# Half-width last tiles and first tiles around three stage borders, in a float32 hybrid layer: the order of matmuls, weight splits, statistics and gate rows is changed

## The reference

```
h = rms_norm(x) * (1 + sc0) + sh0
x = x + 0.5 * g0 * rms_norm(swiglu(h, f_in[0], f_out[0]))      # d_ff 2816
h = rms_norm(x) * (1 + sc1) + sh1
y = token_mixer(h)     # h @ w_in, then mLSTM (8 heads) and attention (16/4 heads), gates, @ w_out
x = x + g1 * rms_norm(y)
h = rms_norm(x) * (1 + sc2) + sh2
x = x + 0.5 * g2 * rms_norm(swiglu(h, f_in[1], f_out[1]))
```

## Time and profile before

| | |
|---|---|
| median of 3 executions | 1885.39 us (1884.95 to 1885.58) |
| the profiled execution | 1890.55 us, span in the trace 1888.7 us |
| busy share of the span | PE 96%, DVE 51%, ACT 35% |
| mean granted TensorE clock | 0.984 of full speed |
| chain that ended last | PE 88%, DVE 5%, ACT 4% |

### The profile page before, as it was taken

The page is one execution under the profiler, slowest core; times in us unless marked ns, Lnnn a source line. Parts: engine busy times, 40 slices in busy tenths (PEclk is TensorE's granted clock), DMA queues, the critical chain, the costliest instruction groups (busy, mean ns, idle before and its releaser), DMA issues.

```text
span 1888.7 us, 31491 instructions
## 1 busy us (share of the span) xinstructions
PE 1808.8 (96%) x12852; PEld 1750.3 (93%) x12852; DVE 967.3 (51%) x1636; ACT 655.9 (35%) x1145; POOL 0.2 (0%) x4
## 2 busy tenths in 40 slices
PE   7899999999988999899999999979999999999997
PEld 6899999999977999899999888879989999999996
DVE  4665555656365334455537888865463212222235
ACT  3422222212364222443435555443652222221233
POOL 0000000000000000000000000000000000000000
PEclk9999999999999999999999999999999999999998
DMA  7444444443213123232243211102312222222221
GB/s 300 154 153 126 156 132 146 131 136 120 70 34 134 57 68 92 87 92 74 91 134 111 66 40 53 38 19 79 134 45 68 77 78 70 75 78 78 66 58 56
DMA packets 52285, 178.35 MB, mean 94 GB/s; under 512 B 8513, under 2 KB 11091, under 8 KB 51411
## 3 DMA queue, kind: packets, MB, share of 16 engines
q1 hardware_dynamic: 52179, 176.86, 29.3%
HBM read 162.28 MB, written 13.90 MB: 93 GB/s over the span
## 4 chain that ended last, share of the span: by engine, by line
PE 88%; DVE 5%; ACT 4%; issue 2%; DMA 0%; SPq 0%; DVEq 0%; ACTq 0%
PE psum L525 21%; PE psum L526 21%; PE psum L527 21%; PE psum L938 2%; PE psum L948 2%; PE psum L913 2%; PE psum L563 1%; PE psum L565 1%; PE psum L564 1%; PE psum L620 1%; PE psum L609 1%; PE psum L653 1%; PE psum L830 1%; PE psum L654 1%; PE psum L655 1%
## 5 line engine op out<-in xcount | busy, mean ns | idle before, releaser
L525 PE MATMUL psum<-h_hi,whi 128*128 128x320 f32 x2096 | 659.6, 315 | 7.9 <-ACT mq L1249 4.5
L527 PE MATMUL psum<-h_hi,wlo 128*128 128x320 f32 x2096 | 650.7, 310 | 0.0
L526 PE MATMUL psum<-h_lo,whi 128*128 128x320 f32 x2096 | 650.7, 310 | 0.0
L1460 DVE TENSOR_TENSOR wlo<-raw,whi 128x1024 fp32r<-128x1024 f32 x191 | 233.2, 1222 | 650.6 <-ACT whi L1042 650.5
L525 PEld LDWEIGHTS psum<-h_hi,whi 128*128 128x128 f32 x2096 | 396.7, 189 | 13.6 <-issue 10.7
L526 PEld LDWEIGHTS psum<-h_lo,whi 128*128 128x128 f32 x2096 | 396.6, 189 | 0.6
L527 PEld LDWEIGHTS psum<-h_hi,wlo 128*128 128x128 f32 x2096 | 396.2, 189 | 0.0
L1042 ACT CAST whi<-raw 128x1024 fp32r<-128x1024 f32 x191 | 199.3, 1044 | 357.9 <-PE psum L527 343.7
L525 PE MATMUL psum<-g_hi,whi 128*128 128x320 f32 x512 | 158.5, 310 | 0.0
L526 PE MATMUL psum<-g_lo,whi 128*128 128x320 f32 x512 | 158.2, 309 | 0.0
L527 PE MATMUL psum<-g_hi,wlo 128*128 128x320 f32 x512 | 158.2, 309 | 0.0
(11 more groups left out here) (329 smaller groups left out, 2619.3 us busy)
## 6 DMA issues: line engine op xcount, KB each, us to landing
raw<-in_w_ffn_in SPq DMA_DIRECT2D x88, 512.0 KB, 3.5
raw<-in_w_mix SPq DMA_DIRECT2D x77, 512.0 KB, 3.9
mw<-in_w_mod SPq DMA_DIRECT2D x28, 768.0 KB, 4.5
raw<-in_w_ffn_out SPq DMA_DIRECT2D x32, 512.0 KB, 3.5
mw<-in_w_mod SPq DMA_DIRECT2D x4, 2048.0 KB, 19.4
gate<-gate_keep SPq DMA_DIRECT2D x24, 320.0 KB, 4.6
mw<-in_w_mod SPq DMA_DIRECT2D x14, 512.0 KB, 3.6
gate_keep<-gate SPq DMA_DIRECT2D x20, 320.0 KB, 4.5
```

Of the source, the lines that this page charges most:

```text
L525: mm(out, whi[t.slot][:, k, :], hi[:, k, cols], start=(k == 0), stop=False)
L526: mm(out, whi[t.slot][:, k, :], lo[:, k, cols], start=False, stop=False)
L527: last = mm(out, wlo[t.slot][:, k, :], hi[:, k, cols], start=False, stop=(k == nk - 1))
L1460: tt(lo[:, 0:nk, :], raw[t.raw][:, 0:nk, :], hi[:, 0:nk, :].bitcast(F32), ALU.subtract).then_inc(raw_free, 1)
```

## The change

Four edits. (a) In `last_tiles` on PE, tiles 0 and 1 are interleaved in their first half: k = 0 to nk - 2 of tile 0, the same of tile 1, then the last k of tile 0, the last k of tile 1. (b) ACT and DVE split the weights one tile further ahead: tile 2 before the loop, then tile i + 3 ahead of the eviction of tile i; the order of the second halves becomes 4, 5, 6, 7, 0, 1, 2, 3, and the kept weights change places (tiles 2 and 3 now in `xhi`/`xlo`). (c) For l < 2, `half_stats_y(l, 1)` is issued inside `first_four`, behind k = 3 of the two interleaved tiles, and all eight calls of `half_stats(l, 1)` behind u = 2. (d) Gate rows: ACT does the Exp behind the eviction of tile 2 and the Ln behind that of tile 3; DVE does `forget()` ahead of the split of tile 5.

```
-SECOND = (2, 3, 4, 5, 0, 1, 6, 7)
+SECOND = (4, 5, 6, 7, 0, 1, 2, 3)
+Y_STATS = 3
...
-            if u >= 6:
-                return xhi[u - 6], xlo[u - 6]
-            return held_r3[u - 4] if l == 1 and u >= 4 else held[u - 2]
+            if u < 4:
+                return xhi[u - 2], xlo[u - 2]
+            return held_r3[u - 6] if l == 1 and u >= 6 else held[u - 4]
...
             def last_tiles(l, base, nk, hi, lo, ready, first):
-                for u in range(KC):
-                    half_tile(l, u, u, base, 0, nk, hi, lo, ready if u == 0 else None, first)
+                for ks in (range(nk - 1), range(nk - 1, nk)):
+                    for u in range(2):
+                        if ks.start == 0:
+                            half_wait(l, u, u, base, 0)
+                        half_passes(l, u, u, base, 0, ks, nk, hi, lo, ready if u == 0 else None, first)
+                for u in range(2, KC):
+                    half_tile(l, u, u, base, 0, nk, hi, lo)
...
-                half_stats_y(l, 1)
+                if l == 2:
+                    half_stats_y(l, 1)
...
                             last = first_half(l, base, u, h, range(k, k + 1), u == 0)
                             if h == 1 and k == KC - 1:
                                 last.then_inc(tile_done, 1)
+                        if h == 0 and k == Y_STATS:
+                            half_stats_y(l, 1)
...
                         if h == 0:
-                            half_stats(l, 1, range(4 * u - 8, 4 * u - 4))
+                            if u == 2:
+                                half_stats(l, 1, range(KC))
...
+                split(w[2], weights(l, 2, base)[0], w[0].n + 2, nk)
                 for i in range(KC):
-                    u = i + 2
...
+                    u = i + 3
                     if u < KC:
                         split(w[u], weights(l, u, base)[0], w[0].n + 2, nk)
                     square_y(l, i, 0, base)
...
-                if l == L_GATE + 1:
+                if l == L_GATE + 2:
                     act.wait_ge(row_d, 1)
                     fn(t1[:, :, :], t1[:, :, :], ACT.Exp, scale=-1.0).then_inc(row_a, 1)
+                if l == L_GATE + 3:
                     act.wait_ge(row_a, 1)
                     fn(t1[:, :, :], t1[:, :, :], ACT.Ln, bias=epsc[0:H, 1:2]).then_inc(row_a, 1)
...
+                split(w[2], weights(l, 2, base), nk)
                 for i in range(KC):
-                    if i + 2 < KC:
-                        split(w[i + 2], weights(l, i + 2, base), nk)
+                    if i + 3 < KC:
+                        split(w[i + 3], weights(l, i + 3, base), nk)
                     take(i, 0)
...
+                if l == 1:
+                    forget()
                 if l < 2:
                     split(Tile(T_MIX + l + 4))
```

More of the change, by code:

```diff
@@ L174, in build @@
         whole = KC * P * 4
-        held = [[at(f"held{u}_{n}", [P, KC, P], F32R, h_at + (u - 2) // 2 * KC * row + (u % 2 * 2 + n) * whole)
-                 for n in range(2)] for u in range(2, 6)]
+        held = [[at(f"held{u}_{n}", [P, KC, P], F32R, h_at + (u - 4) // 2 * KC * row + (u % 2 * 2 + n) * whole)
+                 for n in range(2)] for u in range(4, KC)]
         held_r3 = [[at(f"held_r3_{u}_{n}", [P, KC, P], F32R, r3 + (u % 2 * 2 + n) * whole)
-                    for n in range(2)] for u in range(4, 6)]
+                    for n in range(2)] for u in range(6, KC)]
         xtok = at("xtok", [P, NT, D], F32, h_at)
@@ L548, in project_two, with half_wait @@
                             last.then_inc(tile_done, 1)
-            def half_tile(l, i, u, base, h, nk, hi, lo, ready=None, first=0):
+            def half_wait(l, i, u, base, h):
                 t, w = Tile(base + i), Tile(base + u)
-                wh, wl = weights(l, u, base)
                 if h == 0:
@@ L558, in half_tile, with half_passes @@
                     pe.wait_ge(ev[t.slot], t.pair)
-                out = half_out(t.slot, h)
-                for k in range(nk):
+            def half_passes(l, i, u, base, h, ks, nk, hi, lo, ready=None, first=0):
+                wh, wl = weights(l, u, base)
+                out = half_out(Tile(base + i).slot, h)
+                for k in ks:
                     if ready is not None:
@@ L565, in half_tile @@
                     last = mm(out, wl[:, k, :], hi[:, k, HCOLS[h]], start=False, stop=(k == nk - 1))
-                last.then_inc(tile_done if h else h0_done, 1)
-            def last_tiles(l, base, nk, hi, lo, ready, first):
-                for u in range(KC):
-                    half_tile(l, u, u, base, 0, nk, hi, lo, ready if u == 0 else None, first)
+                if ks.stop == nk:
+                    last.then_inc(tile_done if h else h0_done, 1)
+            def half_tile(l, i, u, base, h, nk, hi, lo):
+                half_wait(l, i, u, base, h)
+                half_passes(l, i, u, base, h, range(nk), nk, hi, lo)
+            def last_tiles(l, base, nk, hi, lo, ready, first):
+                for ks in (range(nk - 1), range(nk - 1, nk)):
[5 more added lines that the diff above has]
+                    half_tile(l, u, u, base, 0, nk, hi, lo)
                 for i, u in enumerate(SECOND):
@@ L1113, in first_split @@
                     split(Tile(nxt + u), first_weights(u, nxt)[0], Tile(done_by).n + 3)
+                act.wait_ge(mod_mul, 2 * KC * MOD_LATER)
+                if l == 1:
+                    act.wait_ge(misc_st, 16 * 7)
+                split(w[2], weights(l, 2, base)[0], w[0].n + 2, nk)
                 for i in range(KC):
-                    u = i + 2
[L1116 to L1119, removed]
+                    u = i + 3
                     if u < KC:
@@ L1831, in _ @@
                     ts(t_pair[:, :, :].rearrange("h d n -> h (d n)"), cst[0:H2, 0:2 * N], 0.0, None, ALU.mult).then_inc(nm_zero, 1)
-                if l == 1:
-                    forget()
                 if l in (2, 3, 4):
```

## The result

| | before | after |
|---|---|---|
| median of 7 executions each, same chip | 1885.39 us (1884.72 to 1887.08) | 1873.37 us (1868.53 to 1878.35) |
| ratio of the two | | 0.9936 (0.9922 to 0.9950) |
| the profiled execution | 1890.55 us | 1873.35 us |
| its span and mean granted clock | 1888.7 us, 0.984 | 1871.5 us, 0.988 |

The change takes 12.0 us from the median, where 18.4 were forecast. The time is inside the range and 6.4 us above the predicted 1867.0. From trace to trace it takes 17.2 us. So the total of the traces came out within 1.2 us, and the step from a trace to the median did not; most of what follows is about these two facts. The closeness of the first is in part luck: at the places that the forecast has terms for, the traces differ by 16.3 us, 1.6 come from a stretch that it has no term for, and the start took 0.8 longer.

The account below looks back on a forecast made before the run. PE, busy 96% of the span, was the bound, leaving its idle and low-clock time: 0 + 7.8 + 5.2 + 5.4 + 0 = 18.4 us off 1890.55 gives 1872.1, median 5.2 lower: 1867.0 us; range 1862.5 to 1875.

Parts of the forecast that it names:

- First halves: Borders 0 and 2, edits (a) and (b): DVE's 3.40 us loop, not PE, sets the pace, so 0.0 gained.
- End of border 0: Edit (c): ACT's root of x starts earlier and the wait for h_lo goes; 7.8 us gained, bounds 0 to 10.5.
- Gate rows: Edit (d): eviction wait of 4.5 and low clock go, 7.3, less 2.1 longer wait at turn_gates: 5.2 us gained.
- Border 1: ACT's root of x 4.9 us earlier, plus 0.5 for the low clock: 5.4 gained, 0.4 from a small wait included.
- wait inside the block of statistics: Rival 1, both borders: late squares make PE wait among the eight statistics, about 3 us gained each, 1874.2; chance 0.10.
- reappearing 4.5: Rival 4: half_stats_y behind 24 matmuls delays y by 3.5 at both borders, 4.5 reappear; 7.0 slower, 1892; chance 0.03.
- raw loads: Rival 5: the earlier weight splits wait on raw loads, making the edits neutral, 1885; chance 0.03.
- the median lies 5.2 lower: Final step from the profiled execution, forecast at 1872.1 us, to the median: 5.2 us lower, giving 1867.0.
- 2.0, if the low clock comes back in this wait: Lower bound of the gate rows' gain: low clock returns in the longer wait at turn_gates; 5.2 was taken.
- Rival 3: First halves of borders 0 and 2: the clock swings, up to 5.3 us a half, 15 us in all, 1882; chance 0.04.
- Rivals 3 and 5: Clock swings in first halves, 1882, chance 0.04; earlier splits waiting on raw loads, neutral at 1885, chance 0.03.
- within: Whole kernel: change in time inside about 0.2%, 3.8 us, which a measurement can't tell from no change; chance 0.03.

Follow-up runs that it names:

- s_take: Whole change plus DVE's eviction take(i) ahead of the split of tile i + 3 in the first halves; 1863.03 us, ratio 0.9879 to the kernel before.
- t_fill: Whole change plus idle matmuls of constants on PE in its waits; 1869.60 us, ratio 0.9917 to the kernel before.
- r_stats: Only edit (c), the moved statistics of y and x, on the kernel before; 1881.11 us, ratio 0.9972.
- r_first: Only edits (a) and (b), interleaved first tiles and earlier weight splits, on the kernel before; 1885.82 us, ratio 1.0000.
- s_late: Whole change plus turn_gates one tile later on PE; 1873.18 us, ratio 0.9925 to the kernel before.
- r_rows: Only edit (d), the gate rows, on the kernel before; 1883.19 us, ratio 0.9981.
- t_both: Whole change plus eviction ahead of split on DVE and turn_gates one tile later on PE; 1863.46 us, ratio 0.9872 to the kernel before.
- s_y: Only the statistics-of-y half of edit (c) on the kernel before; 1883.21 us, ratio 0.9992.
- t_cd: Edits (c) and (d) together, without (a) and (b), on the kernel before; 1875.33 us, ratio 0.9944.

## Why the prediction was right, and where it failed

**Term by term**, from trace to trace. First halves: 0 forecast, -0.1 at each measured; the argument that DVE's loop and not PE sets them holds. End of border 0: 7.8 against 5.9; 1.5 of the difference is the low clock behind the wait of 2.16, which my sum had at the higher clock. Where it did not fall (s_take, t_fill) the term is 30.52 - 23.48 + 0.37 = 7.4. Gate rows: 5.2 against 5.8 with the clock in it. The size was near, for a reason that is partly wrong: I booked 2.6 for the low clock behind the wait of 4.5. In r_stats and r_first the same wait has a shorter fall behind it (11 and 14 matmuls at the lower clock's spacing, 21 in before), and tile 4 to turn_gates needs 23.06 and 23.17 us. After needs 23.11 with no fall at all, because its turn_gates waits 1.8 for the rows, where r_stats waits

```profile
PE psum L760 <- ACT gm L1277: 0.3, 1, 0.3
```

So such a short fall only covers time in which PE would have waited. With the wait of 4.5 gone as well, d is worth 34.8 - 30.15 = 4.6 from an execution with the short fall and 5.8 from one with the long one. Border 1: 5.4 against 4.8; of the 0.4 in its first halves the traces show 0.05 (31.14 to 31.09 us). The rivals on the order of work don't show: no wait inside the block of statistics, no reappearing 4.5, no raw loads.

**The step that failed**, for the size of the gain, is "the median lies 5.2 lower". I took the difference between the profiled execution of before and its median over to the kernel after unchanged. The executions of before mostly lie at a mean clock of 0.986 to 0.988, the profiled one at 0.984: it had falls of the clock that the typical one has not, the change was credited with taking them out, and then the 5.2 were taken off again. After's profiled execution, 1873.35, happens to be its median, so the offset is zero there, and 17.2 - 5.2 = 12.0.

No typical execution of before was traced. The nearest stand-in is r_first, which has its median (1885.82) and a profiled execution of 1885.24 at 0.987. By the table, from r_first to after: the end of border 0 brings 29.56 + 8.65 - 25.00 - 7.70 = 5.5, the gate rows 11.71 + 23.17 - 7.04 - 23.11 = 4.7, border 1 24.67 + 8.65 - 20.71 - 7.71 = 4.9, and behind turn_gates after loses 13.03 - 9.98 = 3.1 to the clock. That is 12.0 in sum, and 1885.24 - 1873.35 = 11.9. So the gap to the forecast has places: 1.5 behind the wait for the split, 3.1 behind turn_gates, and some 2 that I had taken from the falls of one execution. The fall behind turn_gates was a bound of mine ("2.0, if the low clock comes back in this wait"), and the gate rows are then worth 4.7 - 3.1 = 1.6, beside 2.6 in the medians for d alone. I had set the likeliest value at the end without a fall. Three reservations: that r_first looks like a typical execution of before is argued from its time, not traced; each length is from one execution; and t_fill and s_late show that what is saved there isn't all kept.

**Rival 3**, the clock swinging in the first halves, came halfway. The fall is there, behind the first long wait (0.94 in 503:534), but it cost nothing there, because it hit a single half tile and the loop absorbed it; it cost 1.5 at the end of border 0. The Trainium skill ("TensorE: Matmul & The Clock Gate", A second HAM failure mode: psum-queue depth-cycling) says that frequent small idle times between groups of matmuls degrade throughput by such swings. This case's traces show no swing from small waits: the one fall in the first halves of after comes behind a single wait of 2.12, and in r_rows the first halves have five y waits of 0.36 to 0.99 and the wait of 2.64 with a clock of 1.00 from 503 to 534. I had the rival at 0.04 by one stretch of one execution, whose longest wait was 0.79, and which starts just behind a fall in the same trace (0.57 from 507 to 511, above).

**A slip in the chances.** Rivals 3 and 5, at 1882 and 1885, both lie within 3.8 us of the time before, so the chance of "within" should have been 0.07 and not 0.03.

## What to carry to other kernels

An eviction written behind the weight split of a later tile waits for everything that the split waits for: look for a loop of two in-order engines whose period is longer than PE's work for a tile, and take one hand-over out of it, before interleaving matmuls around it. Here the swap of two calls was worth 10.3 us on top of the 12.0 of the whole change (in the traces, 1.5 of them hang on a fall of the clock behind the wait for the split, which t_both has with the same swap). Work moved forward into a wait pays only if the chain that ends last later waits for that engine. And before a difference of traces is carried to a median, compare the mean granted clock of the profiled execution with that of the timed ones, and price the low-clock time apart.

## What the runs showed of the hardware

The clock fell behind a wait of 2.12 us at border 0 and behind one of 2.16 some 60 us later in the same execution, and not behind the same wait of 2.2 in s_take, s_y and t_cd. Behind the wait of 4.5 it fell in all six traces that have this wait, though not for equally long: in r_stats

```profile
602.04 0.61 PE L526 MATMUL psum<-h_hi,whi 128*128 128x320 f32 x1 [4.51 <-ACT mq L1254]
602.45 0.47 PE L527 MATMUL psum<-h_lo,whi 128*128 128x320 f32 x1
...
605.30 0.31 PE L526 MATMUL psum<-h_hi,whi 128*128 128x320 f32 x1
```

11 matmuls were spaced by more than 0.2 us, in before 21. So the price of such a wait isn't set by its length alone. Executions of one program on one core differ by up to 9.8 us (after: 1868.53 at 0.992, 1878.35 at 0.984), which is about 1.2 us for 0.001 of mean clock. The mean clock does not tell everything: among the executions of before at 0.987 are 1884.75 and 1887.59 us, and one of 1890.33 has 0.937. What makes these differ is open.
